# Second branch's gate as block products in the convolution stage; the first attention with two projections a pair

## The reference, cut to what matters

```python
def hybrid_layer(x, norm_g, w_in, conv_w, q_norm_g, k_norm_g, sinks, w_conv_out, w_attn_out, gate_b, w_out):
    h = rms_norm(x, norm_g)
    u = jnp.einsum('bsd,dc->bsc', h, w_in)
    v_c, b_c, c_c, z_c, q, k, v, z_a, gate_logits = jnp.split(u, SPLIT_POINTS, axis=-1)
    y_c = b_c * causal_depthwise_conv(c_c * v_c, conv_w)
    y_c = y_c * jax.nn.silu(z_c)
    y_a = jnp.einsum('bsc,cd->bsd', y_c, w_conv_out)
    q = rms_norm(q.reshape(b, s, 16, 64), q_norm_g)
    k = rms_norm(k.reshape(b, s, 4, 64), k_norm_g)
    o = sliding_window_attention(q, k, v, sinks) * jax.nn.silu(z_a)   # window 128, sinks in the softmax
    y_b = jnp.einsum('bsc,cd->bsd', o, w_attn_out)
    g_a, g_b = jnp.split(jax.nn.sigmoid(gate_logits + gate_b), 2, axis=-1)
    merged = g_a * y_a + g_b * y_b
    return x + jnp.einsum('bsd,de->bse', merged, w_out)
```

## Time and profile before

| | us |
|---|---|
| median of 3 runs (2691.53 to 2696.58) | 2694.8 |
| the profiled execution | 2693.12 |
| its span | 2691.3 |
| TensorE busy in the span | 2586.6 |
| stage of 16 block pairs (102.0 to 411.4) | 309.4 |
| first attention (586.35 to 1002.43) | 416.1 |

### The profile page before, as it was taken

The page is one execution under the profiler, slowest core; times in us unless marked ns, Lnnn a source line. Parts: engine busy times, 40 slices in busy tenths (PEclk is TensorE's granted clock), DMA queues, the critical chain, the costliest instruction groups (busy, mean ns, idle before and its releaser), DMA issues.

```text
span 2691.3 us, 37487 instructions
## 1 busy us (share of the span) xinstructions
PE 2586.6 (96%) x12094; PEld 2089.5 (78%) x12094; DVE 1418.6 (53%) x2044; ACT 1057.7 (39%) x1923; POOL 1327.3 (49%) x1100
## 2 busy tenths in 40 slices
PE   8999999999999989999999999899999999999989
PEld 5788888877777778888878888676778888787777
DVE  5455543135655565435555555636776656714445
ACT  4333331065545541116777777612433332401121
POOL 3788873331222124431111111456578787577766
PEclk9999999999999999999999999999999999999999
DMA  3222224311111014321111111222222222533333
GB/s 103 83 78 64 69 95 169 117 38 40 39 47 39 32 48 148 109 68 52 40 40 39 39 39 40 75 98 79 90 78 83 81 82 78 176 118 125 121 129 118
DMA packets 101630, 215.57 MB, mean 80 GB/s; under 512 B 11152, under 2 KB 11280, under 8 KB 101536
## 3 DMA queue, kind: packets, MB, share of 16 engines
q1 hardware_dynamic: 74432, 135.82, 16.1%
q10 hardware_dynamic: 27104, 78.56, 8.2%
HBM read 177.57 MB, written 36.77 MB: 80 GB/s over the span
## 4 chain that ended last, share of the span: by engine, by line
PE 77%; DVE 7%; ACT 6%; issue 5%; DMA 2%; POOL 2%; ACTq 0%; DVEq 0%; POOLq 0%; SPq 0%
PE bank L629 18%; PE bank L692 17%; PE bank L918 14%; PE flip L918 7%; PE pv L918 3%; PE flip L1079 3%; PE bank L1105 3%; PE pv L1079 3%; PE pv L863 2%; DMA raw<-in_w 2%; POOL wlo L533 1%; PE score L835 1%; PE flip L848 1%; POOL whi L531 1%; PE score L832 1%
## 5 line engine op out<-in xcount | busy, mean ns | idle before, releaser
L531 POOL TENSOR_SCALAR whi<-raw 128x512 fp32r<-128x512 f32 x350 | 258.6, 739 | 1211.6 <-PE bank L692 724.5
L533 POOL TENSOR_TENSOR wlo<-raw,whi 128x512 fp32r<-128x512 f32 x350 | 501.4, 1433 | 29.2
L629 PE MATMUL bank<-b_lo,whi 128*128 128x512 f32 x496 | 198.0, 399 | 2.3 <-DVE b_hi L2016 2.3
L629 PE MATMUL bank<-a_hi,whi 128*128 128x512 f32 x464 | 184.9, 399 | 3.4 <-POOL wlo L533 2.0
L692 PE MATMUL bank<-b_hi,whi 128*128 128x512 f32 x384 | 154.9, 403 | 5.6 <-DVE fk_lo_odd L2114 3.2
L546 POOL TENSOR_TENSOR wlo<-a,whi 128x512 fp32r<-128x512 f32 x102 | 148.2, 1453 | 15.3 <-ACT whi L1473 15.3
L629 PE MATMUL bank<-b_hi,whi 128*128 128x512 f32 x368 | 147.8, 402 | 8.1 <-DVE b_lo L1984 6.6
L692 PE MATMUL bank<-a_hi,whi 128*128 128x512 f32 x368 | 149.1, 405 | 6.3 <-DVE s_z L2061 5.1
L692 PE MATMUL bank<-b_hi,wlo 128*128 128x512 f32 x384 | 151.5, 395 | 0.0
L692 PE MATMUL bank<-b_lo,whi 128*128 128x512 f32 x384 | 151.2, 394 | 0.0
L692 PE MATMUL bank<-a_lo,whi 128*128 128x512 f32 x368 | 145.6, 396 | 0.0
(11 more groups left out here) (528 smaller groups left out, 7234.8 us busy)
## 6 DMA issues: line engine op xcount, KB each, us to landing
raw<-in_w SPq DMA_DIRECT2D x350, 256.0 KB, 2.6
a<-in_pairs SPq DMA_DIRECT2D x136, 256.0 KB, 2.6
h_scr<-up_y ACTq DMA_DIRECT2D x22, 512.0 KB, 2.6
fc<-c_scr ACTq DMA_DIRECT2D x16, 512.0 KB, 3.6
stage<-h_scr ACTq DMA_DIRECT2D x22, 256.0 KB, 3.4
a<-h_scr ACTq DMA_DIRECT2D x21, 256.0 KB, 3.4
y_scr<-up_y ACTq DMA_DIRECT2D x8, 512.0 KB, 2.6
t_scr<-y_room ACTq DMA_DIRECT2D x8, 512.0 KB, 2.9
```

What stands on the lines that cost most here:

```text
L531: nc.gpsimd.tensor_scalar(hi, src, 1.0, 1.0, ALU.mult, ALU.mult).then_inc(w_hi, 1)
L533: nc.gpsimd.tensor_tensor(lo, src, hi.bitcast(F32), ALU.subtract).then_inc(w_lo, 1)
L629: last = nc.tensor.matmul(psum_ap, ws[w][:, k, :], a[:, kt, hs(h)], start=(first and i == 0 and j == 0), stop=(final and i == n - 1 and j ...
```

## The change

- The 8 units of the second branch's gate leave the attention and become 4 pairs of block products in the convolution stage, ahead of the last two pairs of the first gate: `NC` goes from 16 to 20. ScalarE makes their tanh (`branch_pair`) at the head of the next pair and stores them (`branch_store`).
- The attention's pairs keep two units: queries and `z_a`. The next pair's `scores(0)` with its maxima, exponentials and scaling moves ahead of this pair's `values(3)`. The second half of a unit is cut into 5 and 3 tiles around values and scores.
- The last pair keeps one unit, and the first products of the output projection (`merge_part`, into the score banks) begin in it: the first four tiles of the inputs of two units come first, the last four behind them.
- `s_sq` gets a room of its own, that of `s_g`.

```diff
-NC = 16
+N_A = 2 * (KT - 1)
+NC = N_A + KT // 2 + 2
...
+            def merge_part(c, h, ks):
+                for k in ks:
+                    if k == 0:
+                        pe.wait_ge(w_lo, (U_AOUT + c) * 2 + 2)
+                        pe.wait_ge(sw.exp, 4 * (NW * NPAIR - 1 + c))
+                    pe.wait_ge(sw.o_lo, k + 1)
+                    last = product(score[c][:, hs(h)], (U_AOUT + c) % 2, b_lo, b_hi, [k], [k], h, k == 0, k == KT - 1)
+                    if k == KT - 1:
+                        last.then_inc(tile_done[h], 1)
...
+                if last_pair:
+                    scores(1)
+                    fill(1, 0)
+                    flip_p(0)
+                    scores(2)
+                    values(0)
+                    flip_p(1)
+                    scores(3)
+                    values(1)
+                    flip_p(2)
+                    fill(1, 1)
+                    values(2)
+                    flip_p(3)
+                    merge_part(0, 0, range(2))
+                    values(3)
+                    return
                 scores(1)
                 fill(0, 0)
                 flip_p(0)
-                fill(0, 1)
+                fill(0, 1, range(5))
+                values(0)
                 scores(2)
-                values(0)
+                fill(0, 1, range(5, KT))
                 flip_p(1)
...
                 scores(3)
+                mean_square(n, 0, bank[0][:], s_sq)
+                pe.wait_ge(sw.q_std, n * 2 + 1)
+                mean_square(n, 1, bank[0][:], s_sq)
                 values(1)
+                fill(1, 0)
                 flip_p(2)
-                fill(1, 1)
+                fill(1, 1, range(5))
                 values(2)
-                fill(2, 0)
+                fill(1, 1, range(5, KT))
                 flip_p(3)
-                fill(2, 1)
+                window_scores(*((it, 1) if pp == 0 else (it + 1, 0)), 0)
                 values(3)
...
+            merge_part(0, 0, range(2, KH))
+            merge_part(0, 1, range(KH))
             for h in range(2):
+                merge_part(1, h, range(KH))
+            for c in range(2):
+                for h in range(2):
+                    merge_part(c, h, range(KH, KT))
...
+                expo(1)
+                act.wait_ge(sw.q_lo, it * 4 + (2 * pp + 6))
+                query(0)
+                high(0)
+                query(1)
                 fold(0)
                 high(1)
...
                 expo(2)
                 fold(1)
+                normed_hi(s_q, n, s_raw)
+                act.wait_ge(sw.og, it * 6 + 3 * pp)
+                gate_a(0)
                 high(2)
                 expo(3)
+                fold(2)
                 gate_a(1)
                 high(3)
+                window_expo(*((it, 1) if pp == 0 else (it + 1, 0)), 0)
                 fold(3)
...
+            def branch_pair(n):
+                act.wait_ge(sums_out, 7 * n + 7)
+                for i, x in enumerate(x_pair[n % 2]):
+                    j = 2 * (n - N_A) + i
+                    nc.scalar.activation(x[:], x[:], ACT.Tanh, scale=0.5, bias=half_gate[:, j:j + 1]).then_inc(gate_made, 1)
...
+            for n in range(N_A + 1, NC - 1):
+                branch_pair(n - 1)
+                conv_high(n + 1, (n + 1) % 2, 0)
+                conv_high(n + 1, (n + 1) % 2, 1)
...
+                copy_first(n, x_pair[n % 2][0])
+                branch_store(n - 1)
+                for pos in range(2, 7):
+                    conv_high(n + 1, (n + 1) % 2, pos)
```

More of the change, by code:

```diff
@@ L2066, in gated, with maxima, normalise @@
                     for h in range(2):
-                        dve.wait_ge(tile_out[h], it * 6 + (u0 + 2))
+                        dve.wait_ge(tile_out[h], it * 4 + (u0 + 2))
                     v.scalar_tensor_tensor(s_o[rows, pair, cols], s_o[rows, pair, cols], 0.5, s_z[rows, cols], ALU.mult,
                                            ALU.mult).then_inc(sw.og, 1)
-                maxima(0)
-                normalise(0)
+                def maxima(s):
+                    window_maxima(it, pp, s)
+                def normalise(s):
+                    window_normalise(it, pp, s)
+                if last_pair:
+                    maxima(1)
+                    gate(0)
+                    low(0)
+                    normalise(1)
+                    maxima(2)
+                    add(0)
+                    low(1)
+                    maxima(3)
+                    normalise(2)
+                    add(1)
+                    low(2)
+                    normalise(3)
+                    window_lo(0)
+                    gate(1)
+                    add(2)
+                    window_lo(1)
+                    gated(head_rows[0], slice(0, S), 2)
+                    low(3)
+                    window_lo(2)
+                    gated(head_rows[1], hs(0), 3)
+                    window_lo(3)
+                    add(3)
+                    gated(head_rows[1], hs(1), 4)
+                    return
+                following = (it, 1) if pp == 0 else (it + 1, 0)
                 maxima(1)
-                if last_pair:
-                    gate(0)
                 low(0)
                 normalise(1)
-                if last_pair:
-                    window_lo(0)
-                    window_lo(1)
                 add(0)
@@ L2083, in window_pair @@
                 low(1)
+                maxima(3)
+                normed(n, C_QG, s_raw, s_sq)
                 normalise(2)
-                if not last_pair:
-                    gate(0)
                 add(1)
-                maxima(3)
-                if not last_pair:
-                    normed(n, C_QG, s_raw, s_sq)
+                gate(0)
                 low(2)
+                normed_lo(n, s_q, s_raw)
                 normalise(3)
+                add(2)
                 gate(1)
-                add(2)
-                if last_pair:
-                    window_lo(2)
-                    window_lo(3)
-                else:
-                    normed_lo(n, s_q, s_raw)
+                low(3)
+                window_maxima(*following, 0)
                 gated(head_rows[0], slice(0, S), 2)
                 gated(head_rows[1], hs(0), 3)
-                low(3)
+                window_normalise(*following, 0)
                 add(3)
@@ L2419, in _ @@
+            for c in range(2):
+                merged(0, c, [score[c][:, hs(h)] for h in range(2)])
+            with dve.Fori(1, KT // 2) as it:
+                for c in range(2):
+                    merged(it, c, [bank[h][:] for h in range(2)])
             x_ins = (x_in0, x_in1)
```

289 lines of the change are left out of this document (141 added, 148 removed).

## The result

| | before | changed |
|---|---|---|
| median | 2692.26 (5 runs, 2691.41 to 2696.58) | 2708.78 (5 runs, 2706.51 to 2712.78) |
| the profiled execution | 2693.12 | 2712.78 |
| its span | 2691.3 | 2710.6 |
| stage of block products | 309.4 | 386.6 |
| first attention, and its seven periods | 416.1, 368.3 | 354.7, 312.5 |

A forecast was written before the change was run, and what follows sets the result against it. TensorE, busy 96% of the span, was taken as the bound, so its waits decide. 77.3 - 57.4 - 1.0 - 8.3 - 1.7 = +8.9 us gave 2702.0 or 2703.7, forecast 2703, range 2689 to 2714.

The forecast's parts named there:

- the three signs named: Forecast wrong if the s_raw wait is under 1 us, a steady pair below 43, or the block stage has any gap.
- its own forecast: Whole kernel: the waits come as worked through, +5.5 to +13 us; chance 0.46.
- rival 4: Steady attention pairs: TensorE's clock falls behind new gaps, 2.3 us a pair, 2719, or 2708 for one in three; chance 0.11.
- Rival 5: Block stage: tanh ahead of the conversions makes GpSimd late, 1 to 1.5 us a pair, 2708; chance 0.08.
- Part 1: Block stage: the gate's eight units as four pairs of 19.34 us, without a new wait, +77.3 us.
- Part 2: Steady attention pairs: 48 products fewer but longer waits, 52.8 to 44.6 us, seven pairs -57.4; first pair -1.0 more.
- The shared port: Steady pair: gated products take 0.69, not 1.81, as GpSimd's split has ended; a 2 us slip would make the sum +17.
- Part 3: Last attention pair: 23.3 us of work, 12.4 of waits and 1.3 for the clock, 37.0 against 43.86, -8.3 us.
- Part 4: Start of the output projection: 36 products of the first four tiles come first and shorten waits of 3.3 us, -1.7.

The follow-up runs named there:

- e3: The changed kernel with, in the last pair alone, ScalarE's fold(0) and high(1) ahead of exponentials 2: 2702.9 us.
- e1: The changed kernel with ScalarE's copy and square of the query's first half ahead of exponentials 1: 2697.6 us.
- e2: The changed kernel with ScalarE's gate_a(0), the tanh of z_a's first half, ahead of the two head copies: 2704.8 us.
- e7: The changed kernel with the swaps of e1, e2 and e3, plus scores(2) ahead of values(0) and fold(0) ahead of query(1): 2678.4 us.
- e5: The changed kernel with the next pair's first scores back behind values(3), their exponentials, maxima and normalise likewise moved back: 2738.0 us.
- e6: The changed kernel with its steady pair in the old kernel's order on all three engines, still two projections a pair: 2744.8 us.
- e10: e7 with 32 unused bytes left free in front of the large tensors, no other edit: 2687.6 us.
- e9: e8 with the early logarithm's output put beside another constant, so that no tensor lies elsewhere than in e7: 2670.1 us.
- e8: e7 with the logarithm's table loaded early, through a new one-column tensor, and the first mean square ahead of scores(3): 2679.0 us.

## Why the prediction was right, and where it was off

The direction and the range held, and so did the three signs named: the wait for `s_raw` is over 1 us, a steady pair over 43, the block stage without a gap. The size did not: +16.5 us in the median lies outside the +5.5 to +13 that the prediction called its own forecast. That rivals 4 and 5 had priced 2708 is luck, since neither is what happened in that size. The sum forecast +8.9 on the profiled execution; its span grew by 19.3. The difference by the prediction's own parts:

- **Part 1: +77.3, measured +77.2.** No gap, full clock. The tanh at the head of a pair and the late conversions cost nothing, though GpSimd is busy 318 of 387 us. Rival 5 falls.
- **Part 2: -57.4 and -1.0, measured -55.7** (368.3 to 312.5; the lead-in to the first pair's scores(1) is 0.3 longer). The five waits foreseen were 2.0, 1.95, 1.4, 0.35 and 0.5 a pair; measured, as the totals over seven, 2.1, 1.8, 1.1, 0.2 and none. Five pairs take 44.5 against the forecast's 44.6. The shortfall of 2.7 has two causes. 1.3 is the prediction's base: seven times 52.8 is 369.6, and the seven periods before were 368.3. The other is rival 4 in two of the seven: the clock halves at 692.3 and 723.0, shortly behind the logarithm's and the `s_raw` wait. The first two periods take 43.9 and 46.0, and in e3, with the same order and no fall, 43.4 and 44.4: 2.1 us for two falls, where rival 4 had 2.3 for each. The five pairs without a fall give back 0.1 each.

```profile
719.80:723.00 3.20, 1.01 (x6) 0.69 (x5) 0.00 (x0) 3.17 (x12) 0.00 (x0) 1.00 0.00 0
723.00:726.40 3.40, 3.40 (x10) 2.65 (x9) 2.76 (x5) 0.89 (x2) 0.00 (x0) 0.50 0.02 5
```

  TensorE was busy 1.01 of the 3.20 us ahead of the fall, and then had full work at 1.2 GHz. By the rule of the Trainium skill cited with rival 4 (TensorE: Matmul & The Clock Gate, Part 1) this is how it should look. Why the later pairs, with the same waits, keep 2.4 GHz, no run here settles.
- **The shared port.** In the steady pairs the gated product of 64x512 now takes 0.69 where it took 1.81 and 1.26 on average, and no row of 1.81 is left. The price of 0.69 was right. By the rule of the Trainium skill cited in Part 2 (SBUF — State Buffer, "SBUF: two separate sides") that follows from GpSimd's split having ended by then. The trace agrees: the split ends at 803.30 and the gated products start at 803.25.

```profile
L2068 DVE SCALAR_TENSOR_TENSOR s_o<-s_o,s_z 64x512 f32 x12 | 15.1, 1255 | 0.4
```

```profile
L2124 DVE SCALAR_TENSOR_TENSOR s_o<-s_o,s_z 64x512 f32 x12 | 8.3, 689 | 0.4
```

  In the last pair, where the prediction looked for none, the same two engines now meet. GpSimd's subtraction takes 2.14 us instead of 1.29, and beside it VectorE's product of 64x1024 takes 2.30 instead of the 1.21 that it took before. The low parts that `values(3)` waits for come behind it:

```profile
1014.47 2.14 POOL L533 TENSOR_TENSOR wlo<-raw,whi 128x512 fp32r<-128x512 f32 x1
...
1015.38 2.30 DVE L2124 SCALAR_TENSOR_TENSOR s_o<-s_o,s_z 64x1024 f32<-64x1024 f32 x1
```

- **Part 3: 37.0, measured 37.9.** The waits foreseen were 2.5, 1.0, 3.7, 2.3, 1.3 and 1.6. Measured were 2.07, none, 2.37, 1.79, 1.52 and 1.96: 9.7 instead of 12.4. But TensorE was busy 28.1 us where the working had 23.3 and 1.3 for the clock. The granted 0.91 of 37.9 us is up to 3.4 of it (an estimate: 0.09 x 37.9); the working, which goes from start to start, also leaves out the end of the last product ahead of each wait.

```profile
PE pv L774 <- DVE sp_lo L2106: 6.4, 3, 2.4
PE flip L756 <- DVE sp L2093: 1.8, 1, 1.8
PE score L629 <- DVE b_hi L2070: 1.5, 1, 1.5
```

- **Part 4 was mis-sized: -1.7, with the 1.4 us of work moved into the last pair -3.1; measured -1.2** (193.01 to 191.85). The waits went from 2.3 us, where the prediction had taken 3.3, to 0.3, where it had left 1.6: saved 2.0 against 1.7. What took the gain is again the clock, which falls as the last pair ends. The products behind it take 0.43 us each and not 0.23, which also covers the tiles that come late:

```profile
1013.60:1020.00 6.40, 2.89 (x15) 1.78 (x13) 6.37 (x6) 2.47 (x4) 2.92 (x3) 1.00 0.25 82
1020.00:1026.80 6.80, 6.47 (x15) 4.62 (x15) 6.64 (x8) 4.38 (x5) 0.00 (x0) 0.50 0.00 0
```

- **Outside all parts: +4.7.** 1.9 before the block stage and 2.8 behind the output projection, where the change moves nothing. The first block product starts between 99.8 and 103.9 in the fourteen profiles, and from the end of the attention to the second block stage the eleven kernels with their tensors in place take about 968 to 973.3 us, of which the kernel before has 970.9 and the changed one the most. No edit of the experiments lies there. In the changed kernel's first 104 us the granted clock was 0.95, in those of the kernel before 0.98; of the 2.8 I can only say that it lies within this spread. The 4.7 us are thus no shown effect of the change, and 4.0 us of spread is what parts the profiled execution from its median.

So 8.9 - 0.1 + 3.0 (Part 2, 2.7, and the lead-in 0.3) + 0.9 (Part 3) + 1.9 (Part 4) + 4.7 = 19.3. The mechanism was right, and the term that was too small is mainly one: **the clock stood in the sum with 1.3 us, for the last pair alone, and otherwise as a rival of 0.11, where it takes a little in each stage that waits.** It took 2.1 us in the steady pairs, up to 3.4 in the last pair, and up to 3.4 in the 6.8 us behind it (an estimate: half of that time). The waits themselves, worked from the two engines' orders, were 5.2 us a pair against 6.2. e1, e2 and e7 show the causes, since the swaps took the waits that they were aimed at: `s_raw` 14.6 to none, `s_z` 7.5 to 0.7 (with 4.4 back at the transposes), the logarithm 12.9 to 7.6.

## What to carry to other kernels

- When cover work leaves a pipelined stage, the waits that appear are set by the fixed order of the helper engines: work each order through, then look for an instruction that was ready while its engine idled behind another's wait. Here one swapped line was worth 11 us, and eight such moves together 44 (2708.8 to 2664.7), with no work removed; the falls of the clock that went with the waits are in these numbers.
- Price each wait twice: its length, and the products behind it at half clock. Of what the seven periods grew by, 12 us of 30 in e5 and 14 of 35 in e6 were of the second kind.
- Before a kernel with one more tensor is compared, look at a stage that the edit does not touch.

## What the runs showed of the hardware that was not expected

- **Where tensors lie was worth 0.3 to 0.4% in the block stage.** With the large tensors 32 bytes further, 1681 products of 128x512 at full clock took 388.2 us instead of 386.6; with 64 bytes 387.8. Over the kernel 32 bytes cost 9.2 us (e7 to e10) and 8.9 (e9 to e8), more than most of the swaps; 64 bytes cost 2.4, which is within the noise.
- **The same pair of waits does or doesn't bring the clock down.** The changed kernel's first two steady pairs and e2's first two and last had a fall each; e3's seven, with the same waits as the changed kernel's, had none.
- **A table load costs its 1.28 us and no more** in ScalarE's rows here, and an operation on one column moves it into idle time (e9).
- **VectorE and GpSimd met again where nobody looked, and both were slower.** In the last pair a subtraction of GpSimd took 2.14 us instead of 1.29 and a product of VectorE 2.30 instead of 1.21. Who moves a split in time has to look at what it then stands beside.
